# The second slot of a page step: norms before the dots, sums before the merge, squares before the copy

## The reference, cut to what matters

```
def _decompress(c_kv, w_ukv, g_kn):
    kv = jnp.einsum('btc,chd->bthd', c_kv, w_ukv)
    return _rmsnorm(kv[..., :NOPE], g_kn), kv[..., NOPE:]

def step(carry, phys):
    c_blk = cache_ckv[layer, phys]
    kp_blk = cache_kpe[layer, phys]
    kn_blk, v_blk = _decompress(c_blk, w_ukv, g_kn)
    return _merge(carry, _attn_partial(qn, qp, kn_blk, kp_blk, v_blk, None)), None
```

## Time and profile before

| what | value |
|---|---|
| median of three executions | 1276.44 us (1276.27 to 1277.88) |
| the profiled execution's own time | 1276.86 us |
| its span, first to last instruction | 1275.1 us |
| busy: TensorE, VectorE, ScalarE, GpSimd | 94%, 57%, 33%, 20% of the span |
| mean granted clock of TensorE | 0.984 |

### The profile page before, as it was taken

One profiled execution on the slowest core, in us unless ns is written; L12 is line 12 of the kernel. 1 busy time (PEld: TensorE's weight loads), 2 busy tenths in 40 slices (PEclk: granted clock), 3 DMA queues, 4 the chain that ended last, 5 costly groups with the idle time before them and its releaser, 6 DMA issues. The chain is left out here.

```text
span 1275.1 us, 23690 instructions
## 1 busy us (share of the span) xinstructions
PE 1202.1 (94%) x8783; PEld 661.3 (52%) x8783; DVE 732.2 (57%) x1801; ACT 426.5 (33%) x1041; POOL 257.4 (20%) x294
## 2 busy tenths in 40 slices
PE   6999999989999999999989988999999999989898
PEld 3545677745565565655434445555444444454343
DVE  4000437955667666774768787888676667430331
ACT  3000354323343333342444343333444444210310
POOL 0000134711011121234412340001323232000000
PEclk9999999999999999997999999999999999999999
DMA  6413112123232222351453226532576544101000
GB/s 219 168 55 87 35 33 67 53 59 80 66 81 67 76 73 77 84 115 42 124 143 88 76 74 171 168 80 74 153 184 172 139 122 123 50 1 38 17 21 33
DMA packets 205236, 114.45 MB, mean 90 GB/s; under 512 B 152977, under 2 KB 196433, under 8 KB 204994
## 3 DMA queue, kind: packets, MB, share of 16 engines
q1 hardware_dynamic: 198482, 96.56, 27.7%
q0 software_dynamic: 4352, 10.49, 3.3%
q10 hardware_dynamic: 2288, 5.89, 1.3%
HBM read 75.79 MB, written 4.07 MB: 63 GB/s over the span
## 5 line engine op out<-in xcount | busy, mean ns | idle before, releaser
L563 PE MATMUL PS<-wk,c_T 128*128 128x512 f32 x1024 | 494.5, 612 | 13.5 <-DVE c_T L673 12.4
L563 PEld LDWEIGHTS PS<-wk,c_T 128*128 128x128 f32 x1024 | 180.3, 193 | 207.8 <-issue 162.8
L686 DVE TENSOR_REDUCE ssq<-PS 128x8 f32<-128x512 f32 x256 | 176.3, 689 | 169.7 <-ACT PS L609 156.8
L609 ACT ACTIVATE PS<-PS 128x512 f32<-128x512 f32 x256 | 150.3, 587 | 271.8 <-PE PS L563 245.0
L1557 PE MATMUL PS<-xnT,w_ring 128*128 128x276 f32 x416 | 101.0, 400 | 0.0
L1395 PE MATMUL PS<-w_ring,xnT 128*128 128x424 f32 x256 | 96.4, 534 | 0.9 <-DVE xnT L1041 0.9
L673 DVE STREAM_TRANSPOSE c_T<-blocks 128x512 f32<-128x512 f32 x126 | 88.3, 701 | 3.7 <-DMA blocks<-c_ring 3.2
L1557 PEld LDWEIGHTS PS<-xnT,w_ring 128*128 128x128 f32 x416 | 77.8, 190 | 20.6 <-issue 4.1
L489 POOL DMA_INDIRECT c_ring<-in_cache_ckv,token_rows x48 | 45.3, 944 | 182.1 <-PE PS L547 174.8
L480 POOL DMA_INDIRECT r_ring<-in_cache_kpe,group_rows x64 | 62.0, 969 | 92.3 <-DVE r_T L681 68.0
L1395 PEld LDWEIGHTS PS<-w_ring,xnT 128*128 128x128 f32 x256 | 48.8, 194 | 45.5 <-issue 45.4
(11 more groups left out here) (535 smaller groups left out, 1725.3 us busy)
## 6 DMA issues: line engine op xcount, KB each, us to landing
blocks<-c_ring SPq DMA_DIRECT2D x504, 64.0 KB
c_ring<-in_cache_ckv SPq DMA_DIRECT2D x208, 128.0 KB, 2.2
w_ring<-in_w_in SPq DMA_DIRECT2D x4, 1696.0 KB, 12.4
w_ring<-in_w_in SPq DMA_DIRECT2D x9, 512.0 KB, 5.1
w_o<-in_w_out SPq DMA_DIRECT2D x8, 512.0 KB, 4.9
w_g<-in_w_ple_gate SPq DMA_DIRECT2D x8, 512.0 KB
xn<-in_x_prompt SPq DMA_DIRECT2D x4, 512.0 KB, 10.9
w_ring<-in_w_in SPq DMA_DIRECT2D x2, 1024.0 KB, 6.1
```

The costliest lines, as they stand in the source:

```text
L563: mm = pe.matmul(PS[:, NORM[v % 2], :], c_T[:, u % 2, k, t * P:(t + 1) * P], wk[:, k], start=(k == 0), stop=(k == 1))
L609: nc.scalar.activation(PS[:, NORM[v % 2], :], PS[:, NORM[v % 2], :], ACT.Square).then_inc(no_sb, 1)
L686: dve.tensor_reduce(ssq[:, u % 2, t * H:(t + 1) * H], PS[:, NORM[v % 2], :].rearrange("p (h c) -> p h c", h=H), AX.X, ALU.add).then_inc(re ...
```

## The change

In slot 1 of each step TensorE does `norms(u, 1)` first, and `dots(u)` and `values(u-2)` behind it. ScalarE squares first and copies the dots behind it. VectorE sums first, then merges, then transposes the next rotary keys. `score(u)` waits for one more copy of the dots than before (`np_sb`). No instruction is added or removed, and no buffer changes.

```diff
--- before.py
+++ after.py
@@ -571,13 +571,13 @@
             for u, t in slots:
                 if t == 0 and u >= 2:
                     turn_weights(u - 2)
+                if t == 2 and u >= 1:
+                    turn_scale(u - 1)
+                norms(u, t)
                 if t == 1:
                     dots(u)
                     if u >= 2:
                         values(u - 2)
-                if t == 2 and u >= 1:
-                    turn_scale(u - 1)
-                norms(u, t)
                 yield
             turn_weights(NSTEP - 2)
             yield
@@ -640,11 +640,11 @@
                         turned_weights(u - 2)
                     if u >= 1:
                         roots(u - 1)
-                if t == 1:
-                    dotted(u)
                 if t == 3 and u >= 1:
                     weights(u - 1)
                 square(u, t)
+                if t == 1:
+                    dotted(u)
                 yield
             turned_weights(NSTEP - 2)
             yield
@@ -700,7 +700,7 @@
             def score(u):
                 nm, sc, at = nmax[:, u // STEPS:u // STEPS + 1], score_s[:, u % 2, :], u % 2 * 2 * P
                 dve.wait_ge(rp_ps, min(u + 2, NSTEP))
-                dve.wait_ge(np_sb, u + 1)
+                dve.wait_ge(np_sb, min(u + 2, NSTEP))
                 dve.wait_ge(scale_ps, u + 1)
                 LA(dve.tensor_tensor(sc, sc, PS[:, MISC, at_t], ALU.mult))
                 if u >= 1:
@@ -729,15 +729,16 @@
                     if u >= 1:
                         turned_blocks(u, 1)
                         scales(u - 1)
-                if t == 1 and u >= 2:
-                    merge(u - 2)
                 if t == 2 and u >= 1:
                     score(u - 1)
                 if t == 3 and ahead:
                     turned_blocks(u + 1, 0)
                 reduce(u, t)
-                if t == 1 and ahead:
-                    turned_r(u + 1)
+                if t == 1:
+                    if u >= 2:
+                        merge(u - 2)
+                    if ahead:
+                        turned_r(u + 1)
                 yield
             merge(NSTEP - 2)
             yield
```

## The result

The changed kernel takes 1296.43 us (median of six, 1294.9 to 1299.38) where the kernel before, timed beside it, took 1278.04 (six, 1276.27 to 1283.69): 1.0142 times as long, interval 1.0118 to 1.0166. It is slower, and by more than the range of the forecast allowed. Its profiled execution took 1298.97 us with a span of 1297.2. That is 2.5 over the median; where the total matters I use the medians.

What follows compares the result with a forecast made beforehand. TensorE was taken as the full engine, with the bare stretch's period hanging on when norms 2 starts. Bare stretch +12.8, earlier stages -2.5 and steps beside the prompt's attention +0.2 gave +10.5, 1287.0 us; range 1280.4 to 1293.

Steps and rivals of the forecast that it cites:

- (f): Steps beside the prompt's attention: second sum earlier, merge behind it takes that back; +0.2 us for 8 steps, -2 to +2.
- (e): Stages before the bare stretch: filled dots' waits against new waits for the merge; -2.5 us in all, between -8 and +3.
- (a): Bare stretch, TensorE's slot 1: norms moved first leave nothing between values and scales to cover the merge.
- (b): Bare stretch, merge behind the sum: norms 2 starts later, 0.69 us per step taken, bounds 0.58 and 0.76.
- SP's disturbances: Bare stretch, steps 42 to 63: 2.4 us extra from SP's late queue, to vanish with a period of 9.7.
- (c): ScalarE's square ahead of its copy of the dots: the score's added wait costs nothing, at most 0.27 us.
- (d): SP and POOL: values end 1.7 us later in a step, SP's load has 6.1 in hand, waits stay hidden.
- Fills the dots' waits, at most about 6: Stages before: norms 1 fills up to 1.72 us at each of four places, at most about 6 of 8.1.
- VectorE is free about a microsecond earlier: Stages before, after slot 1: VectorE is free about 1 us earlier, with little of TensorE's waiting to spend it on.
- faster: Rival, chance 0.08: filled waits and earlier VectorE in the stages before win more than the bare stretch loses; 1272.5 us.
- no change: Rival, chance 0.06: restarted scales cost less, or the stages before win some 10 to 12 us; 1277 us.
- the clock falls: Rival, chance 0.03: TensorE's idle spells lower its clock in each of 22 bare steps, +33 us more; 1320 us.

Runs made afterwards that it cites:

- e9: The changed kernel again, unaltered, timed in several rounds against the kernel before on another chip: 1295.77 us, 1.015 times.
- e4: Changed kernel, but the scales of steps 42 to 60 go to another PSUM bank and don't wait for the merge: 1286.04 us (one run).
- e6: Changed kernel with ScalarE's order put back, copy of the dots ahead of the square, and the score's added wait taken back: 1318.0 us (one run).
- e10: Changed kernel with only VectorE's order put back, merge ahead of the second sum, timed in several rounds: 1290.97 us, 1.0113 times the kernel before.
- e5: Changed kernel with VectorE's order back, TensorE doing norms, values, dots, and POOL's gather held until the dots are done: 1265.13 us, 0.9977 times before.
- e7: The kernel before once more, unaltered, one run on the second chip: 1273.06 us, against 1269.22 as that kernel's median there.
- e8: The changed kernel once more, unaltered, one run on the second chip: 1282.42 us, against 1269.22 for the kernel before there.
- e3: Changed kernel with VectorE's order put back and TensorE doing norms, values, then dots: 1320.5 us, 1.0304 times the kernel before.
- e2: Changed kernel with only TensorE's order put back (dots, values, norms), VectorE and ScalarE as changed: 1367.97 us (one run).

## Why the prediction was wrong

The sign and the mechanism of the bare stretch were right, the size was not: +10.5 us forecast, +18.4 measured (1296.43 - 1278.04; 18.6 in e9, 1295.77 - 1277.22). Of the 7.9 us of the miss, 1.8 lie in the bare stretch, 0.6 in (f), and by subtraction 5.5 in (e), which was forecast at -2.5 and comes out at 18.4 - 14.6 - 0.8 = +3.0.

- **(a) and (b), right in mechanism, at their upper bound in size.** The merge ends 969.81 - 964.33 = 5.48 us into the step (5.47 worked out), the scales wait for it, norms 2 starts at 5.76, 0.69 later than before: the value taken. But the third square is at 7.74 instead of 6.99, 0.75 later, because it starts a little later behind a TensorE that has stood still. That was named as the upper bound. (The lower one, 0.58, is 0.56 by its own terms: 957.99 + 0.05 + 0.11 - 957.59.) e4 shows that the wait is all of it.
- **SP's disturbances** went as said, nearly: 206.08 - 21 x 9.79 = 0.5 us are left of 2.4. Bare stretch in sum: 13.87 for 21 periods and 0.75 for step 63, +14.6 instead of +12.8, inside its bounds.
- **(c), right.** The order on ScalarE costs nothing, and e6 shows what it saves (1318.0 us without it).
- **(d), right.** No wait for values or gathers came up.
- **(e) is the step that failed.** "Fills the dots' waits, at most about 6" was right to a tenth: 8.1 became 2.1. The new wait was priced at 0.69 in seven adjacent places, up to 4.8 with part of it swallowed. It measured 12.5 more, in ten places with 3.2 the longest. The error was to carry a price over from the bare stretch, where VectorE is free and both inputs of the merge arrive together, into stages where VectorE or ScalarE is behind with a section's work. There the merge's place in the queue counts: behind the sum it waits for the square, for ScalarE and for that engine's section, and nothing on TensorE covers it. 5.4 of the 12.5 are VectorE's order (e10 against e9), and that order is also what costs: without it the kernel is 4.8 us shorter. The other 7 stay with VectorE's order back, and up to step 42 they are paid by the waits that were filled. "VectorE is free about a microsecond earlier", the gain I set against it, did reach TensorE, but with about 1 us in all: its wait for L673 is 3.0 in e9 and 4.0 in e10. The clock was put at a gain of up to 1.5 us, and it went the other way: from step 20 to 41 TensorE is busy for 2.2 to 6.8 us longer in the changed kernel (e9 against the first trace of before, and the first pair). Why the clock is lower there stays open.
- **(f), near enough.** From step 33 to 41 the changed kernel takes 121.2 us instead of 120.4: +0.8 instead of +0.2. "The merge behind it takes that back" was too little: VectorE's order costs 1.6 there (121.1 in e9, 119.5 in e10).
- **The range** is a second place that failed. Each term came out inside its own bounds, +14.6 of at most 15.2, +3.0 of at most 3, +0.8 of at most 2; added up, the upper bounds give 1276.44 + 20.2 = 1296.6. The stated 1293 took 13.5 for the bare stretch and 3 for (e) and (f) together, on the ground that the extremes would not coincide. They nearly did.

Of the rivals, "faster" and "no change" fell by the same waits, "the clock falls", which was about the bare stretch, by the window at 1.00. The gain that "faster" wanted is there, but for e5, which has the filled waits without the new one in the bare stretch (ahead of it 6.0 us of it are left at four places).

Open are two things ahead of the bare stretch. One is what moves step 20 by up to 13 us from one trace to another (549.72 to 563.14), whatever the kernel; so up to step 42 the difference is +7.3 in the first pair, +4.3 for e9 against the first trace of before, and -1.0 in e7 and e8. On that last chip the changed kernel's single run (1282.42) is 13.2 over the median of the kernel before, less than the 18.4 and 18.6 elsewhere. The other is the lower clock from step 20 on.

## What to carry to other kernels

When an instruction is moved ahead on a full engine, ask what it covered where it stood: here it hid a merge of another engine that the next instruction had to wait for, and with the cover gone even a wait of 0.7 us costs nearly 15 us over 22 rounds. Price such a wait once more in every stage with other neighbours, by the latest input of the engine it hangs on; the clean stretch gives its lower bound. This holds for an engine that is not full as well: VectorE is busy for 57%, and its order alone cost 4.8 us. And before giving up a good reordering, look for another cover (e5: the dots themselves) or another buffer (e4).

## What the runs showed of the hardware

- An indirect gather on POOL that starts beside small column-tiled matmuls goes with their results being ready late: 1.71 us behind the recorded end in e3, 0.07 in e5, where only the gather's start differs (they ran on two chips, each timed against the kernel before). Over the kernel it is 1320.5 against 1265.13 us, or 1.0304 against 0.9977 times before.
- Idle spells of 0.70 and 0.26 us in a period of 9.79 leave TensorE's clock at 1.00 for over 200 us, and so do spells of 1.65 and 0.26 in a period of 10.74 (e6, 1.00 from 902.27 to 1128.20). In e2, with a spell of 1.88 us in each step, it falls to its lower level in every second one. In e7 it fell once in the bare stretch, behind a single spell of 2.09 us.
- From step 20 to 41 the same matmuls kept TensorE busy for 312.23 to 319.54 us from trace to trace, with the granted clock at 0.97 and 0.95.
- The same kernel reached step 42 at 898.28 and 890.26 us in its two traces, with mean periods in the bare stretch of 9.15 and 9.28; the changed kernel reached it at 905.61, 902.57 and 889.26 with 9.81 to 9.82 in all three traces.
